# Channels on the partitions in the first product of five feed-forwards

## The chip, the cores and the metric

The kernel runs on one core of one Trainium2 chip. The metric is device time in microseconds (us), the median of several runs. Lower is better.

## The reference, cut to what matters

Two transformer blocks stand one behind the other, on 256 tokens of width 1024. They hold seven gated feed-forwards with an inner width of 2816:

```
def swiglu_ffn(h, w_in, w_out):
    a, u = jnp.split(h @ w_in, 2, axis=-1)       # 256 x 2816 each
    return (jax.nn.silu(a) * u) @ w_out          # 256 x 1024
```

The first two (first block, one for each layer) take `rmsnorm(x) @ w_ffn_in`. The other five (second block) take `swiglu_ffn(modulate(x, shift, scale), w_in, w_out)`: one on 256 context tokens, four on the latent tokens. All is float32. Beside this, the second block needs a table of modulation rows (a vector times a large matrix, here called ada), which the kernel computes piecemeal during the feed-forwards.

## The kernel before, in words

Every product is made of three TensorE passes to keep float32 precision: an operand is split into a high part in float32r and the rest, `lo = value - hi`, and the product is hi·hi + hi·lo + lo·hi. For weights, ScalarE (ACT) makes `w_hi` from the landed block `land` (L858) and GpSimd (POOL) makes `w_lo` (L766, two halves). For activations, `h_hi` and `h_lo` hold the 1024 input channels on the partitions (8 chunks `k`) and the 256 tokens on the free axis; `hid_hi` and `hid_lo` hold the inner activations in the same way (22 chunks of 128 channels).

Weights are streamed in units of 128 x 1024 float32 (512 KB), in a ring of 4 slots (`RING`). The SyncE queue (SP) issues the transfers in order and waits on `lo_ready` of the unit three before. ACT splits unit u when unit u-4 has been used (`w_used`), then POOL follows, then TensorE (PE).

The first product of a feed-forward (`ffn_in`) runs over 11 groups (`FG`) of 256 inner channels. A group takes 4 units; each unit holds two chunks k, and of each chunk 256 gate columns and 256 up columns. In `product` (L1977 to L1979) the activations are the stationary operand (128 channels x 128 tokens) and 512 weight columns are the moving one. So a group is 4 units x 2 chunks x 2 token tiles x 3 passes = 48 matmuls of 512 columns, into one PSUM bank (2 KB of each partition) per token tile; groups alternate between the bank pairs (0, 2) and (1, 3). The result has tokens on the partitions. ACT applies silu to the gate half (L993, two instructions), VectorE (DVE) multiplies with the up half into `hid` (L1556 or L1559, `gate`) and signals `taken`. Then PE turns `hid` with four 128x128 transposes (L2174, `turn_hid`), which it does one group late, after the next group's matmuls; ACT copies the turned bank to `hid_hi` (L999, `split_hid`) and DVE subtracts to make `hid_lo` (L1448, `turned_lo`).

Groups 1 to 10 run in a hardware loop, two per turn (`my.turns`). In the context feed-forward and in the first latent one, each turn also does one piece of the ada table: DVE sums eight scaled blocks (`ada_sums`, L1892, L1895), PE adds over the partitions (`ada_sum`, L2539 and L2540), DVE adds the bias (`ada_rows_out`, L1915), and SP loads the next blocks (L567), which wait on `ada_steps`, the count of DVE's steps.

The second product (`ffn_out`) has 22 units, each 12 matmuls of 512 columns over the four banks 0 to 3. It begins with three units on banks 1 and 3 alone (`HALF_FIRST`), because banks 0 and 2 are still being read for group 10; it waits on `taken`, then does the other half of the three units and turns the last `hid`.

Each engine's waits are counted by `Known`: `my.at(s, v)` is the value of semaphore `s` to wait for, and `my.up(s)` is an increment.

Of the kernel before, what the change touches and what calls it, by code (L numbers as in the profile page):

```python
# [25 lines left out]
P = 128  # L26
# [172 lines left out]
def build(nc, ins, out):  # L199
    ctx = ExitStack()  # L200
    with ctx:
# [231 lines left out]
        def forward(stages):  # L433
# [9 lines left out]
            for l in range(DEPTH):  # L443
# [29 lines left out]
                do("ffn_out", f"w_ffn_out{l}", ada=ADA_OUTS, columns=0 if last else None, then=dict(src="io", mod=(1, 0)) if last else None)  # L473
# [70 lines left out]
        def _(sp):  # L544
# [144 lines left out]
            def ffn_out(w, ada=(), columns=None, then=None):  # L689
# [150 lines left out]
        def _(act):  # L840
# [142 lines left out]
            def ffn_in(w, rms=False, ada=False, aside=False):  # L983
# [19 lines left out]
                with my.turns((FG - 1) // 2, units=8, w_used=8, taken=2, hi_ready=8, silu_ready=2, turned=2, split_hi=2,  # L1003
                              **{f"landed{s}": 32 for s in range(RING)}) as i:
# [5 lines left out]
                split_hid(FG - 1, slice(2 * (FG - 1), 2 * FG))  # L1010
# [82 lines left out]
            def ffn_out(w, ada=(), columns=None, then=None):  # L1093
# [210 lines left out]
        def _(dve):  # L1304
# [240 lines left out]
            def ffn_in(w, rms=False, ada=False, aside=False):  # L1545
# [17 lines left out]
                if aside:  # L1563
# [4 lines left out]
                            **{f"ada_in{j}": 16 for j in range(4)}) if ada else {}  # L1568
                with my.turns(times, silu_ready=2, w_used=8, taken=2, split_hi=2, split_lo=2, **sums) as i:
# [11 lines left out]
            def ffn_out(w, ada=(), columns=None, then=None):  # L1581
# [363 lines left out]
        def _(pe):  # L1945
# [222 lines left out]
            def turn_hid(g):  # L2168

                pe.wait_ge(sems["taken"], my.at("taken", n["taken"]))  # L2170
# [8 lines left out]
            def ffn_in(w, rms=False, ada=False, aside=False):  # L2179
# [5 lines left out]
                with my.turns(times, units=8, lo_ready=8, w_used=8, taken=2, split_lo=2, turned=2, **sums):  # L2185
                    for g in range(2):
                        pe.wait_ge(sems["taken"], my.at("taken", n["taken"] - 1))
                        group((1 - g, 3 - g), GW)
                        turn_hid(g)
                        n["taken"] += 1  # L2190
                    if ada:
                        ada_sum()
                        ada_at[0] += times - 1

            def ffn_out(w, ada=(), columns=None, then=None):
# [6 lines left out]
                pe.wait_ge(sems["taken"], my.at("taken", n["taken"] - 1))  # L2202
# [5 lines left out]
                pe.wait_ge(sems["taken"], my.at("taken", n["taken"]))  # L2208
                for k in range(first):
                    part(u + k, k, {0: (0,), 1: (0,)}).then_inc(*my.up("w_used"))  # L2210
                turn_hid(FG - 1)
# [417 lines left out]
```

## Time and profile before

| | |
|---|---|
| runs | 2320.15 us median of 3 (2317.98 to 2320.23) |
| the profiled execution's own time | 2314.6 us |
| its span, first to last instruction | 2312.8 us |
| mean granted TensorE clock | 0.983 of 2.4 GHz |
| PE matmul busy | 2160.7 us, 93% |
| PE weight load busy | 1747.6 us, 76% |
| POOL busy | 1700.0 us, 74% |
| ACT busy / DVE busy | 1077.4 us, 47% / 985.8 us, 43% |

The span is one execution taken by the hardware profiler. A matmul's record covers its latency: records of neighbours overlap, so the time that one costs is read from the distance between starts (its pitch) and not from its own duration. What lies outside the span is 1.8 us.

### The profile page before, as it was taken

How to read it: one execution, taken by the hardware profiler on the slowest of the kernel's cores; microseconds unless marked ns; L12 is line 12 of the kernel's file. 1: busy time of each engine (PE TensorE's matmuls, PEld its weight loads, DVE VectorE, ACT ScalarE, POOL GpSimd, SP SyncE). 2: the span in 40 equal slices, each digit the busy share in tenths (PEclk: the TensorE clock that was granted, in tenths of full speed). 3: DMA queues.
4: the chain of work that ended last, by engine and by line, in shares of the span. 5: the costliest groups of instructions: out<-in, count | busy, mean ns of one | idle time of the engine just before them, and what ended most of it. 6: DMA issues, size and time to landing. Idle time of an engine off the chain costs nothing.

```text
span 2312.8 us, 32414 instructions
## 1 busy us (share of the span) xinstructions
PE 2160.7 (93%) x10191; PEld 1747.6 (76%) x10191; DVE 985.8 (43%) x1888; ACT 1077.4 (47%) x1659; POOL 1700.0 (74%) x1367
## 2 busy tenths in 40 slices
PE   5998899999998998899999999999999999979996
PEld 4787778778877787788778777787887787766885
DVE  5555576753555454444544434454113210444112
ACT  4464344345654443444454354555444443434442
POOL 5645388777454886698888879727986988767985
PEclk9999999999999999899999999999999999999998
DMA  6434277765343778587787865524665656444663
GB/s 209 136 120 158 91 282 263 242 201 162 116 149 121 279 255 288 197 300 258 264 282 263 295 204 154 159 78 141 192 203 155 183 186 212 138 153 147 191 207 100
DMA packets 135703, 447.10 MB, mean 193 GB/s; under 512 B 22507, under 2 KB 28099, under 8 KB 135609
## 3 DMA queue, kind: packets, MB, share of 16 engines
q1 hardware_dynamic: 128920, 426.62, 56.0%
q10 hardware_dynamic: 6688, 19.23, 2.5%
q8 instruction: 58, 0.95, 0.2%
q14 instruction: 37, 0.30, 0.0%
HBM read 444.60 MB, written 3.03 MB: 194 GB/s over the span
## 4 chain that ended last, share of the span: by engine, by line
POOL 48%; issue 29%; PE 19%; DVE 1%; POOLq 1%; ACT 0%; DMA 0%; SPq 0%; ACTq 0%; DVEq 0%
POOL w_lo L766 48%; PE ps L1977 5%; PE ps L1978 5%; PE ps L1979 5%; PE ps L2438 1%; PE ps L2403 1%; PE ps L2426 1%; PE ps L2255 1%; POOLq L183 0%; PE ps L2399 0%; POOLq L764 0%; PE ps L2369 0%; PE ps L2174 0%; PE ps L2371 0%; DVE mstat L1738 0%
## 5 line engine op out<-in xcount | busy, mean ns | idle before, releaser
L766 POOL TENSOR_TENSOR w_lo<-land,w_hi 128x512 fp32r<-128x512 f32 x1308 | 1664.0, 1307 | 554.1 <-ACT w_hi L858 552.9
L858 ACT ACTIVATE w_hi<-land 128x1024 fp32r<-128x1024 f32 x654 | 691.6, 1060 | 955.7 <-PE ps L1979 706.0
L1977 PE MATMUL ps<-w_hi,h_hi 128*128 128x512 f32 (+1 forms) x1872 | 745.6, 398 | 64.9 <-DVE h_lo L1425 30.8
L1979 PE MATMUL ps<-w_hi,h_lo 128*128 128x512 f32 (+1 forms) x1872 | 732.4, 391 | 0.0
L1978 PE MATMUL ps<-w_lo,h_hi 128*128 128x512 f32 (+1 forms) x1872 | 731.8, 391 | 0.0
L1977 PEld LDWEIGHTS ps<-w_hi,h_hi 128*128 128x128 f32 x1872 | 353.7, 189 | 162.7 <-issue 45.7
L1979 PEld LDWEIGHTS ps<-w_hi,h_lo 128*128 128x128 f32 x1872 | 353.5, 189 | 75.4
L1978 PEld LDWEIGHTS ps<-w_lo,h_hi 128*128 128x128 f32 x1872 | 353.8, 189 | 68.9
L1448 DVE TENSOR_TENSOR hid_lo<-ps,hid_hi 128x512 f32 (+1 forms) x77 | 53.2, 691 | 570.3 <-ACT hid_hi L999 570.3
L1977 PE MATMUL ps<-w_hi,hid_hi 128*128 128x512 f32 x616 | 246.9, 401 | 12.9 <-POOL w_lo L766 12.9
L1978 PE MATMUL ps<-w_lo,hid_hi 128*128 128x512 f32 x616 | 244.7, 397 | 0.0
L1979 PE MATMUL ps<-w_hi,hid_lo 128*128 128x512 f32 x616 | 244.5, 397 | 0.0
L1895 DVE SCALAR_TENSOR_TENSOR ps<-ada_land,ccol,ps 128x512 f32<-128x512 f32 x322 | 230.5, 749 | 12.9 <-DMA ada_land<-ada_w_dram 4.1
L1977 PEld LDWEIGHTS ps<-w_hi,hid_hi 128*128 128x128 f32 x616 | 116.5, 189 | 45.0 <-POOL w_lo L766 16.2
L1979 PEld LDWEIGHTS ps<-w_hi,hid_lo 128*128 128x128 f32 x616 | 116.4, 189 | 28.5
L1978 PEld LDWEIGHTS ps<-w_lo,hid_hi 128*128 128x128 f32 x616 | 116.5, 189 | 27.5
L1638 DVE SCALAR_TENSOR_TENSOR ps<-ps,rows 128x512 f32<-128x512 f32 x28 | 18.6, 693 | 114.6 <-PE ps L1979 114.6
L1081 ACT ACTIVATE h_hi<-ps 128x512 fp32r<-128x512 f32 x56 | 33.1, 597 | 67.9 <-DVE ps L1416 40.2
L1977 PE MATMUL ps<-w_hi,m_hi 128*128 128x512 f32 x128 | 53.0, 414 | 4.7 <-POOL w_lo L766 3.3
L1915 DVE TENSOR_TENSOR ada_o<-ps,ada_b 2x512 f32<-2x512 f32 x36 | 24.2, 673 | 65.1 <-PE ps L2540 65.1
L1425 DVE TENSOR_TENSOR h_lo<-ps,h_hi 128x512 fp32r<-128x512 f32 x56 | 37.8, 689 | 31.6 <-ACT h_hi L1081 30.7
L1978 PE MATMUL ps<-w_lo,m_hi 128*128 128x512 f32 x128 | 50.6, 396 | 0.0
(265 smaller groups left out, 1916.7 us busy)
## 6 DMA issues: line engine op xcount, KB each, us to landing
land<-ffn_w_in_dram SPq DMA_DIRECT2D x220, 512.0 KB, 3.6
ada_land<-ada_w_dram SPq DMA_DIRECT2D x144, 512.0 KB, 5.2
land<-ffn_w_out_dram SPq DMA_DIRECT2D x110, 512.0 KB, 3.9
land<-w_ffn_in_dram SPq DMA_DIRECT2D x88, 512.0 KB, 3.9
land<-w_ffn_out_dram SPq DMA_DIRECT2D x44, 512.0 KB, 4.2
land<-na_w_qkv_dram SPq DMA_DIRECT2D x40, 512.0 KB, 4.1
land<-w_xkv_dram SPq DMA_DIRECT2D x32, 512.0 KB, 3.5
land<-w_in_dram SPq DMA_DIRECT2D x32, 488.0 KB, 3.5
```

Of the source, the lines that this page charges most:

```text
L766: done = pool.tensor_tensor(w_lo[:, slot, half], land[:, slot, half], w_hi[:, slot, half].bitcast(F32), ALU.subtract)
L858: act.activation(w_hi[:, slot, :], land[:, slot, :], ACT.Copy).then_inc(*my.up("hi_ready"))
L1081: act.activation(half_of(h_hi, i), turned_bank(i), ACT.Copy).then_inc(*my.up("split_hi"))
L1425: dve.tensor_tensor(half_of(h_lo, i), turned_bank(i), half_of(h_hi, i).bitcast(F32), ALU.subtract).then_inc(*my.up("split_lo"))
L1448: dve.tensor_tensor(lo_dst, bank(TURN + kp).rearrange("p (a b) -> p a b", a=2), hi_src.bitcast(F32), ALU.subtract).then_inc(*my.up("split_ ...
L1895: ins_ = dve.scalar_tensor_tensor(acc, w, c, acc, ALU.mult, ALU.add)
L1915: dve.tensor_tensor(ada_o[:, :], ps[0:2, ADA_OUT, :], ada_b[:, :], ALU.add).then_inc(*my.up("ada_sum"))
L1977: pe.matmul(dst, lh, wh, start=first, stop=False)
L1978: pe.matmul(dst, lh, wl, start=False, stop=False)
L1979: done = pe.matmul(dst, ll, wh, start=False, stop=last)
L2255: done = pe.transpose(ps[0:m, b, c * SEQ + t * P:c * SEQ + (t + 1) * P], tile, ident[:, :])
L2403: yield pe.matmul(s[:, t * SEQ:(t + 1) * SEQ], q[:, t * P:(t + 1) * P], k, start=(c == 0), stop=(c == len(mp["qk"]) - 1))
```

## The change

In the five feed-forwards of the second block, groups 1 to 10 exchange the operands: the weights become the stationary operand (128 input channels x 128 inner channels) and the 256 tokens of `h_hi` or `h_lo` are the moving one. The result has inner channels on the partitions, as `hid_hi` and `hid_lo` need it, so that the transposes of these groups fall away. A group is now 4 units x 2 chunks x 4 column blocks x 3 passes = 96 matmuls of 256 columns. Gate blocks (c = 0, 1) go to bank g%2, up blocks (c = 2, 3) to bank g%2 + 2. ACT's silu is one instruction of 512 elements; DVE multiplies in place in the up bank; ACT copies that bank to `hid_hi`; DVE subtracts to `hid_lo`. A bank pair is free for the next group when `split_lo` says that `hid_lo` is made, where `taken` said it before. Group 0 stays as it was, with its four transposes after group 1. The first block's two feed-forwards (`rms=True`) stay as they were. DVE's order in the ada turns moves: a turn was sums, group, group, rows out; it is now group, rows out, sums, group, with the first sums and the last rows out outside of the loop.

```diff
@@ PE, ffn_in @@
+                def group_turned(g):
+                    for j in range(4):
+                        u = n["units"]
+                        n["units"] += 1
+                        slot = u % RING
+                        pe.wait_ge(sems["lo_ready"], my.at("lo_ready", u + 1))
+                        for a in range(2):
+                            k = 2 * j + a
+                            for c in range(4):
+                                dst = ps[:, g % 2 + 2 * (c // 2), c % 2 * SEQ:(c % 2 + 1) * SEQ]
+                                at = slice(a * GW + c * P, a * GW + (c + 1) * P)
+                                pe.matmul(dst, w_lo[:, slot, at], h_hi[:, k, :], start=(k == 0 and c % 2 == 0), stop=False)
+                                pe.matmul(dst, w_hi[:, slot, at], h_hi[:, k, :], start=False, stop=False)
+                                done = pe.matmul(dst, w_hi[:, slot, at], h_lo[:, k, :], start=False, stop=(k == KC - 1 and c % 2 == 1))
+                        done.then_inc(*my.up("w_used"))
+                    n["taken"] += 1
+                pe.wait_ge(sems["taken"], my.at("taken", n["taken"] - 1))
+                group_turned(1)
+                turn_hid(0, n["taken"] - 1)
+                n["split_lo"] += 1
+                pe.wait_ge(sems["taken"], my.at("taken", n["taken"] - 1))
+                group_turned(2)
+                if ada:
+                    ada_sum()
+                with my.turns(times - 1, units=8, lo_ready=8, w_used=8, taken=2, split_lo=2, **sums):
                     for g in range(2):
-                        pe.wait_ge(sems["taken"], my.at("taken", n["taken"] - 1))
-                        group((1 - g, 3 - g), GW)
-                        turn_hid(g)
-                        n["taken"] += 1
+                        pe.wait_ge(sems["split_lo"], my.at("split_lo", n["split_lo"]))
+                        group_turned(1 - g)
+                        n["split_lo"] += 1
                     if ada:
                         ada_sum()
@@ PE, ffn_out, not rms: both waits on "taken" become waits on "split_lo", and turn_hid(FG - 1) is left out @@
@@ ACT, ffn_in @@
+                def silu_turned(g):
+                    act.wait_ge(sems["w_used"], my.next("w_used", 4))
+                    act.wait_ge(sems["taken"], my.at("taken", n["taken"]))
+                    n["taken"] += 1
+                    act.activation(flat(sg), bank(g % 2), ACT.Silu).then_inc(*my.up("silu_ready"))
+                def high(g, at):
+                    act.wait_ge(sems["taken"], my.at("taken", n["taken"]))
+                    act.activation(flat(hid_hi[:, at, :]), bank(g % 2 + 2), ACT.Copy).then_inc(*my.up("split_hi"))
...
-                    for g in (0, 1):
+                    for g in (2, 3):
                         split(4)
-                        split_hid(g, bass.ds(i * 4 + 2 * g, 2))
-                        silu(g + 1)
+                        silu_turned(g)
+                        high(g, bass.ds(i * 4 + 2 * g, 2))
@@ DVE, ffn_in @@
+                def gate_turned(g, at):
+                    dve.wait_ge(sems["silu_ready"], my.next("silu_ready"))
+                    n["w_used"] += 4
+                    up = bank(g % 2 + 2)
+                    dve.tensor_tensor(up, up, sg[:, :, :].rearrange("p t n -> p (t n)"), ALU.mult).then_inc(*my.up("taken"))
+                    dve.wait_ge(sems["split_hi"], my.next("split_hi"))
+                    dve.tensor_tensor(hid_lo[:, at, :], up.rearrange("p (a b) -> p a b", a=2), hid_hi[:, at, :].bitcast(F32),
+                                             ALU.subtract).then_inc(*my.up("split_lo"))
...
+                    with my.turns(times - 1, silu_ready=2, w_used=8, taken=2, split_hi=2, split_lo=2, **sums) as i:
+                        gate_turned(2, bass.ds(i * 4 + 4, 2))
+                        if ada:
+                            ada_rows_out()
+                            ada_sums()
+                        gate_turned(3, bass.ds(i * 4 + 6, 2))
```

## Rows read from the trace of the kernel before

**Rows 1.** The page: busy time of each engine, and the chain by engine.

```profile
PE 2160.7 (93%) x10191; PEld 1747.6 (76%) x10191; DVE 985.8 (43%) x1888; ACT 1077.4 (47%) x1659; POOL 1700.0 (74%) x1367
...
POOL 48%; issue 29%; PE 19%; DVE 1%; POOLq 1%; ACT 0%; DMA 0%; SPq 0%; ACTq 0%; DVEq 0%
```

**Rows 2.** Windows, two stages: length; PE, PEld, DVE, ACT, POOL busy; PEclk, DMA, GB/s.

```profile
986.44:1099.77 113.33, 113.33 (x520) 92.99 (x519) 45.80 (x75) 51.73 (x69) 99.26 (x80) 1.00 0.80 278
...
1807.74:1918.74 111.00, 111.00 (x509) 91.73 (x508) 13.54 (x30) 52.26 (x70) 99.22 (x80) 1.00 0.62 189
```

**Rows 3.** Timeline, PE, one group of the fourth stage: start, us, instruction.

```profile
1853.16 0.60 PE L2174 MATMUL ps<-ident,hid 128*128 128x128 f32 x4
...
1855.21 0.39 PE L1978 MATMUL ps<-w_lo,h_hi 128*128 128x512 f32 x1
...
1863.37 0.39 PE L1978 MATMUL ps<-w_lo,h_hi 128*128 128x512 f32 x1
...
1864.51 0.60 PE L2174 MATMUL ps<-ident,hid 128*128 128x128 f32 x4
```

**Rows 4.** Timeline, second product and an ada piece: PE and POOL.

```profile
1110.01 0.40 PE L1977 MATMUL ps<-w_hi,hid_hi 128*128 128x512 f32 x1
...
1110.65 12.74 POOL L766 TENSOR_TENSOR w_lo<-land,w_hi 128x512 fp32r<-128x512 f32 x10 [2.22 <-ACT w_hi L858]
...
1113.51 0.39 PE L1977 MATMUL ps<-w_hi,hid_hi 128*128 128x512 f32 x1
...
1114.21 0.40 PE L2539 MATMUL ps<-ada_hi,pick_r 128*2 128x512 f32 x1
...
1114.45 0.39 PE L2540 MATMUL ps<-ada_lo,pick_r 128*2 128x512 f32 x1
```

**Rows 5.** Timeline, PE, short plain-float32 matmuls in the attentions.

```profile
115.85 1.89 PE L2438 MATMUL ps<-zin,probT 128*128 128x64 f32 x16
...
713.27 1.89 PE L2438 MATMUL ps<-vals,probT_x 128*128 128x256 f32 x8
```

**Rows 6.** Groups by line and shape: busy us, mean ns of one.

```profile
L1979 PEld LDWEIGHTS ps<-w_hi,h_lo 128*128 128x128 f32 x1872 | 353.5, 189 | 75.4
...
L2539 PEld LDWEIGHTS ps<-ada_hi,pick_r 128*2 128x2 f32 x46 | 3.9, 84 | 9.1 <-DVE ada_lo L1904 7.0 <-issue 0.3
...
L2438 PE MATMUL ps<-zin,probT 128*128 128x64 f32 x256 | 30.5, 272 | 0.0
L2438 PE MATMUL ps<-vals,probT_x 128*128 128x256 f32 x64 | 14.8, 379 | 0.0
```

**Rows 7.** Windows and timeline, PE, 512 columns at the low clock.

```profile
925.00:929.00 4.00, 4.00 (x11) 3.12 (x10) 2.90 (x4) 1.26 (x2) 3.96 (x4) 0.50 1.02 410
...
925.28 0.63 PE L1979 MATMUL ps<-w_hi,hid_lo 128*128 128x512 f32 x1
...
929.12 0.63 PE L1979 MATMUL ps<-w_hi,hid_lo 128*128 128x512 f32 x1
```

**Rows 8.** Timeline, fourth stage, end of group 10 and behind it.

```profile
1909.92 0.60 PE L2174 MATMUL ps<-ident,hid 128*128 128x128 f32 x4
...
1911.08 0.58 ACT L999 ACTIVATE hid_hi<-ps 128x512 f32 x1
...
1911.56 0.65 ACT L993 ACTIVATE sg<-ps 128x256 f32<-128x256 f32 x2
1911.83 0.69 DVE L1448 TENSOR_TENSOR hid_lo<-ps,hid_hi 128x512 f32 x1 [10.00 <-ACT hid_hi L999]
```

**Rows 9.** Timeline, first stage, DVE and SP around an ada piece.

```profile
1020.98 0.49 PE L2174 MATMUL ps<-ident,hid 128*128 128x128 f32 x3
...
1024.76 0.73 DVE L1892 TENSOR_SCALAR ps<-ada_land,ccol 128x512 f32<-128x512 f32 x1
1025.53 5.50 DVE L1895 SCALAR_TENSOR_TENSOR ps<-ada_land,ccol,ps 128x512 f32<-128x512 f32 x7
...
1029.30 0.36 SPq L567 DMA_DIRECT2D ada_land<-ada_w_dram  x1
```

More of the change, by code:

```diff
@@ L472, in forward @@
                 last = l == DEPTH - 1
-                do("ffn_out", f"w_ffn_out{l}", ada=ADA_OUTS, columns=0 if last else None, then=dict(src="io", mod=(1, 0)) if last else None)
+                do("ffn_out", f"w_ffn_out{l}", rms=True, ada=ADA_OUTS, columns=0 if last else None, then=dict(src="io", mod=(1, 0)) if last else None)
                 do("rms", FC, gain=None if last else G_MIX + 8 * (l + 1))
@@ L687, in ffn_in, with ffn_out @@
                 stored[0] += times - 1
-            def ffn_out(w, ada=(), columns=None, then=None):
+            def ffn_out(w, ada=(), columns=None, then=None, rms=False):
                 extra = ada_extra([at - 5 for at in ada])
@@ L1091, in make_h, with ffn_out @@
                     high(i)
-            def ffn_out(w, ada=(), columns=None, then=None):
+            def ffn_out(w, ada=(), columns=None, then=None, rms=False):
                 if columns is not None:
@@ L1568, in ffn_in @@
                             **{f"ada_in{j}": 16 for j in range(4)}) if ada else {}
+                def gate_turned(g, at):
[6 more added lines that the diff above has]
+                                             ALU.subtract).then_inc(*my.up("split_lo"))
+                if not rms:
+                    if ada:
+                        ada_sums()
+                    dve.wait_ge(sems["silu_ready"], my.next("silu_ready"))
+                    n["w_used"] += 4
+                    up = bank(3)
+                    dve.tensor_tensor(up, up, sg[:, :, :].rearrange("p t n -> p (t n)"), ALU.mult).then_inc(*my.up("taken"))
+                    turned_lo(hid_lo[:, 0:2, :], hid_hi[:, 0:2, :], 0)
+                    dve.wait_ge(sems["split_hi"], my.next("split_hi"))
+                    dve.tensor_tensor(hid_lo[:, 2:4, :], up.rearrange("p (a b) -> p a b", a=2), hid_hi[:, 2:4, :].bitcast(F32),
+                                             ALU.subtract).then_inc(*my.up("split_lo"))
+                    with my.turns(times - 1, silu_ready=2, w_used=8, taken=2, split_hi=2, split_lo=2, **sums) as i:
+                        gate_turned(2, bass.ds(i * 4 + 4, 2))
+                        if ada:
+                            ada_rows_out()
+                            ada_sums()
+                        gate_turned(3, bass.ds(i * 4 + 6, 2))
+                        if ada:
+                            ada_at[0] += times - 2
+                    gate_turned(FG - 1, slice(FC - 2, FC))
+                    if ada:
+                        ada_rows_out()
+                    return
                 with my.turns(times, silu_ready=2, w_used=8, taken=2, split_hi=2, split_lo=2, **sums) as i:
@@ L1579, in ffn_in, with ffn_out @@
                 turned_lo(hid_lo[:, FC - 2:FC, :], hid_hi[:, FC - 2:FC, :], 0)
-            def ffn_out(w, ada=(), columns=None, then=None):
+            def ffn_out(w, ada=(), columns=None, then=None, rms=False):
                 for at in ada:
@@ L2184, in ffn_in @@
                 sums = dict(ada_split=1, ada_mm=1, ada_sum=1) if ada else {}
-                with my.turns(times, units=8, lo_ready=8, w_used=8, taken=2, split_lo=2, turned=2, **sums):
+                if rms:
+                    with my.turns(times, units=8, lo_ready=8, w_used=8, taken=2, split_lo=2, turned=2, **sums):
+                        for g in range(2):
+                            pe.wait_ge(sems["taken"], my.at("taken", n["taken"] - 1))
+                            group((1 - g, 3 - g), GW)
+                            turn_hid(g)
+                            n["taken"] += 1
+                        if ada:
+                            ada_sum()
+                            ada_at[0] += times - 1
+                    return
@@ L2188, in ffn_in @@
-                        group((1 - g, 3 - g), GW)
-                        turn_hid(g)
-                        n["taken"] += 1
+                        pe.wait_ge(sems["split_lo"], my.at("split_lo", n["split_lo"]))
+                        group_turned(1 - g)
+                        n["split_lo"] += 1
                     if ada:
                         ada_sum()
-                        ada_at[0] += times - 1
-            def ffn_out(w, ada=(), columns=None, then=None):
+                        ada_at[0] += times - 2
@@ L2196, in part, with ffn_out @@
+                n["split_lo"] += 1
+            def ffn_out(w, ada=(), columns=None, then=None, rms=False):
                 def part(u, k, outs):
@@ L2201, in ffn_out @@
                 first = HALF_FIRST
-                pe.wait_ge(sems["taken"], my.at("taken", n["taken"] - 1))
+                if rms:
+                    pe.wait_ge(sems["taken"], my.at("taken", n["taken"] - 1))
+                else:
+                    pe.wait_ge(sems["split_lo"], my.at("split_lo", n["split_lo"] - 1))
                 u = n["units"]
@@ L2207, in ffn_out @@
                     part(u + k, k, {0: (1,), 1: (1,)})
-                pe.wait_ge(sems["taken"], my.at("taken", n["taken"]))
+                if rms:
+                    pe.wait_ge(sems["taken"], my.at("taken", n["taken"]))
+                else:
+                    pe.wait_ge(sems["split_lo"], my.at("split_lo", n["split_lo"]))
                 for k in range(first):
                     part(u + k, k, {0: (0,), 1: (0,)}).then_inc(*my.up("w_used"))
-                turn_hid(FG - 1)
+                if rms:
+                    turn_hid(FG - 1)
                 for k in range(first, FC - 4):
```

29 lines of the change are left out of this document (25 added, 4 removed).

## The prediction

> **What bounds the kernel now.** I began with the page. PE is busy 93% of the span, POOL 74%, and yet the chain that ended last puts 48% on POOL's `w_lo` and 19% on PE [rows 1]. That chain alone would say that POOL is the limit, so the stage has to say who really waits. I laid windows over the five stages, from the first transposes to the last. In all of them PE is busy for the whole window at the full clock (113.33 of 113.33 us, 111.00 of 111.00 us); POOL is busy 99.2 us of 111.00 [rows 2]. So PE never waits, and POOL waits for a slot that PE gives back. POOL's floor is ten halves in 12.74 us, 2.55 us for a unit and 10.2 us for a group [rows 4]; PE needs 11.35 us for a group. PE's own time sets these stages, by a margin of 1.1 us a group.
>
> What is inside of those 11.35 us comes from PE's timeline. Between two transposes 11.35 us pass. Matmuls start at 1855.21 and, 36 of them later, at 1863.37: 226.7 ns each. 48 of these are 10.88 us, and so the turn of `hid` costs PE 0.47 us a group: four transposes, the refilling behind them, and a few slower matmuls [rows 3].
>
> **The change, part by part.**
>
> *The transposes go.* Ten turns in each of five feed-forwards: 50 x 0.47 = 23.5 us off PE. Nothing hides this gain, since PE is the stage's limit.
>
> *48 matmuls of 512 columns become 96 of 256.* The columns that stream are the same; what counts is the cost of one short matmul, x. There are 5 x 10 x 48 = 2,400 pairs, each costing 2x - 226.7 ns more. Break-even for the product alone is x = 113.3 ns; with the 23.5 us of the transposes it is x = 118.2. The trace has no float32r matmul of 256 columns, and this is where the prediction is decided.
>
> Lower bound: at 2.4 GHz 256 columns take 106.7 ns. In plain float32 256 columns take two clocks each: eight in 1.89 us less one duration of 0.379 make 216 ns, 213.3 and 2.5 over, with a weight load behind every one [rows 5, 6]. So a short matmul with a new stationary operand can have as little as 2.5 ns of its own. And loads limit x from below: a load of 128 columns records 189 ns, one of 2 columns 84 [rows 6], so 126 columns are 105 ns and a full load is 107 ns; 16 matmuls of only 64 columns, each with its load, come at 108 ns [rows 5, 6]. So x is at least 108 or 109.
>
> Upper bound: a float32r matmul of 512 columns takes 226.7 ns in the first product [rows 3] and 233.3 ns in the second (15 in 3.50 us, [rows 4]), 13.4 to 20 ns above the 213.3 of the bare stream. If all of this were a fixed price of an instruction, x would be 120.1 to 126.7. If it goes by columns, x is 113.3 to 116.7. What speaks for the columns: at the 1.2 GHz level (granted clock 0.50) nine matmuls take 3.84 us, 426.7 ns each, which is 512 columns and nothing over [rows 7]. The excess is only there when 4-byte columns pass at 2.4 GHz, and plain float32, which takes two clocks for a column, has 2.5 ns only. A limit on the reading of the moving operand does just that. The weight load is not its cause: the ada matmul at 1114.21 has a load of two columns behind it (84 ns) and still 0.24 us to the next [rows 4, 6]. But a fixed gap that the slower clock hides fits as well. I take x = 115.0, the middle of the column case: 2,400 x (230.0 - 226.7) = +8 us.
>
> By the Trainium skill, page "TensorE: Matmul & The Clock Gate", section "Back-to-back issue gap", a matmul costs its columns over 2.4 GHz plus 2.5 ns: 109.2 ns at 256 columns, with which the pairs would save 20 us and not cost 8. For 512 columns that rule gives 215.8 ns where this trace has 226.7 and 233.3, so it is not exact for these operands; the same section says that in a stream of loads and matmuls both set the spacing, with 81 ns at 128 columns where the bare rule has 56. That speaks against the change, since it doubles the loads; 25 ns more on x would cost 120 us.
>
> *Loads double*, from 48 to 96 a group. At 107 ns each they fit behind 113 to 117 ns of streaming, without room to spare. No pair in the trace has both near 107, so this is a risk and not a term.
>
> *ACT and DVE.* ACT: one silu of 512 in place of two of 256 (0.65 us), the same copy (0.58). DVE: two operations of 512 (0.69 each) for two of 256 and one of 512. Both lie beside PE: ACT is busy 52 us and DVE 14 to 46 us of a window [rows 2]. Their order matters where PE waits on them. Behind group 10 in the trace, ACT is free 1.16 us after PE's last matmul (1909.92 to 1911.08) [rows 8]. New: silu 0.60, multiply 0.69, copy 0.58, subtract 0.69, with 0.17 us between engines (1911.66 to 1911.83): `hid_lo` is ready 4.2 us after a group's end. Inside of the loop its bank is wanted again 11 us after, so nothing waits. At the start of the second product it is wanted after 18 matmuls, 18 x 0.233 = 4.2 us: a tie. I put 0.3 us there for wait and refilling, five times: +1.5 us. The three splits that ACT has queued behind need slots which the second product has not given back by then, so they lose nothing.
>
> *The ada pieces in two stages.* DVE's sums began 3.8 us after the group's end (1020.98 to 1024.76). Now they come behind `hid_lo` (4.2) and the rows out (some 0.7), at 4.9: 1.1 us later. SP's next ada load, and the weight transfers queued behind it, need two of the eight steps, which were done at 1026.3; SP issued it at 1029.30, 3.0 us later [rows 9]. So 1.1 us is covered; if that cover were gone the weights' transfers would be late next. Priced at nothing. POOL: at x = 115 a unit is 2.76 us of PE, and POOL's floor stays 2.55.
>
> **Sum**, against the profiled execution's own 2314.6 us: - 23.5 + 8 + 1.5 = - 14, so 2300.6 us. The runs' median is 2320.15, and the same 14 us off it make 2306.
>
> **The rivals.** Times are on the median's footing; without the pair term they start at 2320.15 - 22 = 2298.
>
> *A. The excess goes by columns (my forecast)*, x from 113.3 to 117: pair term 0 to +17.5 us, 2298 to 2316. Chance 0.45.
>
> *B. The excess is a fixed price of each float32r matmul*, x from 119 to 126.7. It speaks for it that the excess varies (13.4, 20) with unchanged columns, which a pure rate would not do. Pair term +27 to +64 us: 2325 to 2362, slower. It decides from x = 118.9 on (0.2% above). Chance 0.32.
>
> *C. Between the two*, x from 117 to 118.9: 2316 to 2325, no change. Chance 0.11.
>
> *D. The excess is a matter of long streams* and vanishes, x from 108.5 to 113, limited by the loads: pair term down to - 23 us, 2275 to 2298. The rows of the attentions speak for it (108 and 216 ns) [rows 5], those of float32r against. This is where the page's 109.2 ns would lie. Chance 0.08.
>
> *E. The loads are not hidden* when load and stream are of the same length, x from 130 to 214: pair term from +80 us, a time of 2378 and more. Against it: every load in the trace is hidden but for at most 20 ns. [...] Chance 0.04.
>
> That the change doesn't do what it says, so that PE waits for `split_lo` in every group, would take a chain of 11 us for the 4.2 us counted above; I leave it out.
>
> **How the numbers follow.** About 0.2% (4.6 us) is what a measurement of this kernel can tell from no change. Faster: A and D, 0.53. Same: C, 0.11. Slower: B and E, 0.36. Predicted 2306, from A. The range for 8 in 10 takes all of A and C, the upper half of D and of B what lies below x = 123.4 (+48 us): 2290 to 2346. A's own range is 2298 to 2316.
>
> **What would show it.** In the profile after: starts of the 128x256 matmuls in the first product, 113 to 117 ns apart (B: 120 or more; D: 112 or less; E: 130 or more); group lengths of 10.9 to 11.2 us in place of 11.35, plus the ada pieces; the transposes of `hid` (7 x 11 x 4 = 308) become 2 x 44 + 5 x 4 = 108; PE still busy for the whole window and POOL's idle time a little smaller; a wait of PE on `hid_lo` only at the head of the second product, below 0.4 us, in five places; SP's ada loads not later than before against PE. The prediction is wrong if x is 119 or more, which I can't exclude from these rows, or if DVE's chain is late in the two ada stages, which would show as PE gaps there and not in the other three.

## The result and the profile after

The changed kernel takes 2324.2 us in the median of 20 runs (2320.34 to 2333.12), the kernel before 2318.18 in 20 runs beside them. The ratio is 1.0028, 95% interval 1.0018 to 1.0038: 6 us slower, with 4.2 to 8.8 us inside of the interval. I had forecast 14 us faster. The profiled execution took 2327.98 us (span 2326.1), 13.4 more than the profiled one of before. Not all of those 13.4 us belong to the change: the first product of the first feed-forward, which the diff leaves alone, already starts 2.0 us later (at 292.2 after 290.2), the second 3.1 us later (751.4 after 748.3), and the first changed one 3.9 us later (965.1 after 961.2), before any changed group has run.

The page of the changed kernel: busy times, and the chain by engine.

```profile
PE 2173.6 (93%) x12391; PEld 1858.0 (80%) x12391; DVE 987.7 (42%) x1838; ACT 1075.7 (46%) x1609; POOL 1701.5 (73%) x1367
...
POOL 49%; issue 30%; PE 18%; DVE 1%; POOLq 1%; ACT 0%; DMA 0%; SPq 0%; ACTq 0%; DVEq 0%
```

PE does 2,200 more matmuls (10,191 before [rows 1]: 2,400 more for the pairs, 200 transposes fewer) and is busy 12.9 us longer. The chain still names POOL for nearly half; as before, that is not where the time went. Groups of the changed kernel by line and shape: busy us, mean ns of one, idle before them.

```profile
L2272 PE MATMUL ps<-h_hi,w_lo 128*128 128x256 f32 x1600 | 454.2, 284 | 6.1 <-POOL w_lo L766 6.1
L2273 PE MATMUL ps<-h_hi,w_hi 128*128 128x256 f32 x1600 | 453.1, 283 | 0.0
L2274 PE MATMUL ps<-h_lo,w_hi 128*128 128x256 f32 x1600 | 453.0, 283 | 0.0
```

1,600 of each line are 4,800 matmuls of 256 columns. Nothing makes them wait but POOL, for 6.1 us in all. Their price is read from the starts. The timeline of PE, fourth stage:

```profile
1812.12 0.28 PE L2272 MATMUL ps<-h_hi,w_lo 128*128 128x256 f32 x1
1812.24 0.28 PE L2273 MATMUL ps<-h_hi,w_hi 128*128 128x256 f32 x1
1812.36 0.28 PE L2274 MATMUL ps<-h_lo,w_hi 128*128 128x256 f32 x1
...
1813.92 0.28 PE L2272 MATMUL ps<-h_hi,w_lo 128*128 128x256 f32 x1
```

From 1812.12 to 1813.92 are 15 matmuls: 1.80 us, **x = 120.0 ns**. A pair costs 240.0 ns where one matmul of 512 columns cost 226.7 [rows 3]. The handover into the second product, where I had put 0.3 us, and the chain of ACT and DVE beside it:

```profile
1922.59 0.28 PE L2274 MATMUL ps<-h_lo,w_hi 128*128 128x256 f32 x1
1922.71 0.39 PE L2040 MATMUL ps<-w_hi,hid_hi 128*128 128x512 f32 x1
1922.94 0.40 PE L2041 MATMUL ps<-w_lo,hid_hi 128*128 128x512 f32 x1
```

```profile
1923.94 0.58 ACT L1020 ACTIVATE sg<-ps 128x512 f32<-128x512 f32 x1
...
1924.55 0.70 DVE L1604 TENSOR_TENSOR ps<-ps,sg 128x512 f32<-128x512 f32 x1 [9.29 <-ACT sg L1020]
1925.28 0.60 ACT L1025 ACTIVATE hid_hi<-ps 128x512 fp32r<-128x512 f32 x1 [0.77 <-DVE ps L1604]
1925.91 0.69 DVE L1606 TENSOR_TENSOR hid_lo<-ps,hid_hi 128x512 fp32r<-128x512 f32 x1 [0.67 <-ACT hid_hi L1025]
```

PE goes from one product into the other without a gap or a refilling, and `hid_lo` is done at 1926.60, 3.9 us after the group's end (I had counted 4.2). It is in time: no matmul behind 1922.71 waits for it. The turns are gone as counted; one tile of the changed kernel, all its matmuls:

```profile
L2237 PE MATMUL ps<-ident,hid x108: 269/272/273, 319.3 to 2141.4; 128*128 128x128 f32 x108
```

Per feed-forward, measured from the first matmul of its first product to that of the stage behind it, the two profiles give 196.7 and 198.3 us for the first of the five, 197.3 and 198.7 for the second, 200.1 and 201.6 for the fourth: +1.4 to +1.6 us each. The third has +3.3. Half of that is the clock: at 1773.87, in its second product, PE had stood 1.49 us for `w_lo`, and from 1774 to 1778 the granted clock was 0.57, where the same stretch of the kernel before has 1.00; 4 us at 0.57 cost 1.7 us. The terms with x = 120.0 say 480 pairs x 13.3 ns = 6.4, less ten turns of 0.47 = 4.7, so +1.7.

### The profile page after: what moved, and what is told of

It reads as the page before. It is cut to its first block, busy times and chain, and to the rows that moved or that the text cites. A ratio compares the mean times of both kernels' runs of the same rounds, so it can differ in the third digit from the quotient of the medians.

```text
span 2326.1 us, 36480 instructions
## 1 busy us (share of the span) xinstructions
PE 2173.6 (93%) x12391; PEld 1858.0 (80%) x12391; DVE 987.7 (42%) x1838; ACT 1075.7 (46%) x1609; POOL 1701.5 (73%) x1367
## 4 chain that ended last, share of the span: by engine, by line
POOL 49%; issue 30%; PE 18%; DVE 1%; POOLq 1%; ACT 0%; DMA 0%; SPq 0%; ACTq 0%; DVEq 0%
POOL w_lo L766 48%; PE ps L2040 3%; PE ps L2042 3%; PE ps L2041 3%; PE ps L2272 2%; PE ps L2274 2%; PE ps L2273 2%; PE ps L2546 1%; PE ps L2534 1%; PE ps L2511 1%; PE ps L2363 1%; POOLq L183 0%; PE ps L2507 0%; POOL ada_land L812 0%; POOLq L764 0%
## 5 line engine op out<-in xcount | busy, mean ns | idle before, releaser
L2040 PE MATMUL ps<-w_hi,h_hi 128*128 128x512 f32 (+1 forms) x1072 | 430.9, 402 | 58.1 <-DVE h_lo L1455 30.9
L2272 PE MATMUL ps<-h_hi,w_lo 128*128 128x256 f32 x1600 | 454.2, 284 | 6.1 <-POOL w_lo L766 6.1
L2273 PE MATMUL ps<-h_hi,w_hi 128*128 128x256 f32 x1600 | 453.1, 283 | 0.0
L2274 PE MATMUL ps<-h_lo,w_hi 128*128 128x256 f32 x1600 | 453.0, 283 | 0.0
L2042 PE MATMUL ps<-w_hi,h_lo 128*128 128x512 f32 (+1 forms) x1072 | 420.8, 393 | 0.0
L2041 PE MATMUL ps<-w_lo,h_hi 128*128 128x512 f32 (+1 forms) x1072 | 420.8, 392 | 0.0
L2272 PEld LDWEIGHTS ps<-h_hi,w_lo 128*128 128x128 f32 x1600 | 307.3, 192 | 9.6 <-issue 5.0
L2273 PEld LDWEIGHTS ps<-h_hi,w_hi 128*128 128x128 f32 x1600 | 307.3, 192 | 0.3
L2274 PEld LDWEIGHTS ps<-h_lo,w_hi 128*128 128x128 f32 x1600 | 307.3, 192 | 0.0
L2042 PEld LDWEIGHTS ps<-w_hi,h_lo 128*128 128x128 f32 x1072 | 203.6, 190 | 43.4
L2041 PEld LDWEIGHTS ps<-w_lo,hid_hi 128*128 128x128 f32 x616 | 117.1, 190 | 27.6
```

The source lines that it names most:

```text
L2040: pe.matmul(dst, lh, wh, start=first, stop=False)
L2041: pe.matmul(dst, lh, wl, start=False, stop=False)
L2042: done = pe.matmul(dst, ll, wh, start=False, stop=last)
L2272: pe.matmul(dst, w_lo[:, slot, at], h_hi[:, k, :], start=(k == 0 and c % 2 == 0), stop=False)
L2273: pe.matmul(dst, w_hi[:, slot, at], h_hi[:, k, :], start=False, stop=False)
L2274: done = pe.matmul(dst, w_hi[:, slot, at], h_lo[:, k, :], start=False, stop=(k == KC - 1 and c % 2 == 1))
```

## The experiments

Twelve kernels. Times in brackets are the kernel before, run beside them. Two theories stood at the start: the *fixed price* (every float32r matmul costs 13.3 ns over its columns, whatever their number; the prediction's B) and the *load* (now that a new stationary tile comes every 120 ns, the load sets the pace or exposes some of itself).

### The price of one matmul by itself

A kernel with TensorE alone: streams of 96 equal matmuls, one kind behind another. It leaves out the whole computation and stores its input.

```
for i in range(N): pe.matmul(ps[:, i % 4, 0:256], st[:, s(i)], xr[:, 0:256], ...)    # L57, also 128, 384, 512 (L55, L59, L61)
for i in range(N): pe.matmul(ps[:, i % 4, 0:256], st[:, 0:P], xr[:, 0:256], ...)     # L63, one stationary tile; 512: L65
for i in range(N): pe.matmul(ps[0:32, i % 4, :], st[:, 32 columns], xr[:, 0:512], ...) # L67
for i in range(N): pe.matmul(ps[:, 0, 0:256], st[:, s(i)], xr[:, 0:256], ...)        # L69, one bank
for i in range(N): pe.matmul(ps[:, i % 4, 0:256], xb[:, s(i)], xb[:, 0:256], ...)    # L73, bfloat16; 512: L75; plain float32: L71
```

> TensorE alone, nothing of the reference is computed (the output is the input x). Stretches of 96 matmuls with start distances: float32r with a new stationary operand each time at 128, 256, 384 and 512 columns; 256 and 512 columns with one stationary operand; 512 columns with a stationary operand of 32 columns; 256 columns into a single bank; plain float32 256; bfloat16 256 and 512. Theory F (the excess is a fixed price of each float32r matmul): 120 at 256, 173 at 384, 227 at 512, the same with one stationary operand and with the narrow one, and bfloat16 only 2 to 3 ns above its stream. Theory L (the price belongs to the weight load of 128 columns, which takes reading away from the stream): 227 at 512 with full loads, 215 to 217 with the narrow stationary operand. Theory C (by columns, my prediction's): 113 at 256, 170 at 384, 227 at 512; it has already lost 256 columns in the changed kernel.

Timeline of that kernel, PE, stretches of a stream: start, us from the first start to the last end, count.

```profile
29.80 1.95 PE L55 MATMUL ps<-xr,st 128*128 128x128 f32 x16
39.82 2.56 PE L57 MATMUL ps<-xr,st 128*128 128x256 f32 x20
54.70 2.59 PE L59 MATMUL ps<-xr,st 128*128 128x384 f32 x14
69.69 2.65 PE L61 MATMUL ps<-xr,st 128*128 128x512 f32 x11
89.80 1.96 PE L63 MATMUL ps<-xr,st 128*128 128x256 f32 x15
109.79 2.43 PE L65 MATMUL ps<-xr,st 128*128 128x512 f32 x10
124.67 2.71 PE L67 MATMUL ps<-xr,st 128*32 128x512 f32 x11
144.74 1.48 PE L69 MATMUL ps<-xr,st 128*128 128x256 f32 x11
169.83 1.46 PE L71 MATMUL ps<-x 128*128 128x256 f32 x6
195.76 2.46 PE L73 MATMUL ps<-xb 128*128 128x256 bf16 x21
209.66 2.54 PE L75 MATMUL ps<-xb 128*128 128x512 bf16 x11
```

The weight loads of the stream with one stationary tile:

```profile
L63 PEld LDWEIGHTS ps<-xr,st 128*128 128x128 f32 x96 | 11.7, 192 | 0.1
```

A stretch less one duration (0.283 us at 256 columns, 0.334 at 384, 0.389 at 512; bfloat16 0.273 and 0.379), over its count less one, is the price. Float32r: 256 columns (2.56 - 0.283) / 19 = 119.8 ns, 384: 173.5, 512: 226.1; over the whole streams the means are 120.5, 173.7 and 227.1. At 2.4 GHz 256, 384 and 512 columns are 106.7, 160.0 and 213.3 ns: the excess is 12.8 to 13.8 for each size, so it is a price of the instruction and not of its columns. One bank: 119.7, so the change of bank does not make it. One stationary tile all along: 119.8 and 226.8, but this says little of the load, since the tile is still loaded ahead of each of the 96 matmuls. What speaks against the load is the size: the excess is the same at 384 and 512 columns, where a load of 107 ns [rows 6] has room to spare, and a stationary tile of 32 columns, whose load is recorded with 109 ns in place of 188, gives not less but 231.6. At 128 columns it is 111.1 ns, where 53.3 + 13.3 would be 67. That fits the load of 107 ns as the limit; no stream without loads was run to show it.

13.3 ns is not the whole price everywhere. The narrow tile has 18 over its columns, and the second products have 20, before [rows 4] and after (233.3 ns at 512 columns). No run here shows what the further 5 to 7 ns are.

Bfloat16: 109.4 and 216.1 (means 109.2 and 215.8), 2.5 over. Plain float32, 256 columns: 216 ns for each of its two passes. The formula of the Trainium skill, page "TensorE: Matmul & The Clock Gate", section "Back-to-back issue gap" (columns over 2.4 GHz and 2.5 ns) agrees with the bfloat16 rows, 109.2 and 215.8; for float32r the measurement decides, and it says 13.3 in place of 2.5.

### Short matmuls with the operands of before

The kernel before, with 480 x 5 matmuls of 512 columns cut in two of 256; the activations stay stationary, and the turns stay.

```
+ for c in range(2):
+     dst = ps[:, b, c * 256:(c + 1) * 256]
+     at = slice(a * GW + c * 256, a * GW + (c + 1) * 256)
+     pe.matmul(dst, lh, w_hi[:, slot, at], ...)
+     pe.matmul(dst, lh, w_lo[:, slot, at], ...)
+     done = pe.matmul(dst, ll, w_hi[:, slot, at], ...)
```

> The kernel before with its operands as they were (activations stationary, transposes kept), but each 512-column matmul of groups 1 to 10 in the five feed-forwards split into two of 256. Theory F (fixed price for each matmul, whichever operand is stationary): 120 ns each, 2,400 x 13.3 = 32 us above before, about 2350. Theory O (the 120 ns come from the exchange of the operands: weights read by the load path, h by the stream): 113 ns each here and no more than before, 2318.

2347.79 us [2318.33], ratio 1.0133 (1.0116 to 1.0150): +29.5 us. 2,400 pairs x 13.3 ns are 31.9. PE's timeline shows the same 120 ns with the other operand stationary:

```profile
1849.82 0.28 PE L2200 MATMUL ps<-w_hi,h_lo 128*128 128x256 f32 x1
...
1850.78 0.28 PE L2199 MATMUL ps<-w_lo,h_hi 128*128 128x256 f32 x1
```

Eight in 0.96 us. Here it does not matter which operand is stationary; that there are two instructions does.

### The turns put back

The changed kernel, with the four transposes of a stale tile behind 40 of the 50 groups.

```
+ for c in range(2):
+     for t in range(T):
+         pe.transpose(ps[:, TURN, ...], hid[:, 0, t, c * P:(c + 1) * P], ident[:, :])
```

> The changed kernel with four transposes of a stale tile put back behind each of groups 3 to 10 of the five feed-forwards, 40 turns (their result is not used). If the turn's price was sized right at 0.47 us, 40 x 0.47 = 19 us above the changed kernel, about 2343. If the transposes had been cheaper than that beside the rest (the alternative for why the change lost), 40 x 0.33 = 13 us or less.

2344.41 us [2318.33], ratio 1.0114 (1.0097 to 1.0131), 20 us above the changed kernel's 2324.2: 0.5 us for a turn, where I had read 0.47 from before. The first term of my sum was right.

```profile
1865.23 0.28 PE L2274 MATMUL ps<-h_lo,w_hi 128*128 128x256 f32 x1
1865.35 0.60 PE L2292 MATMUL ps<-ident,hid 128*128 128x128 f32 x4
1865.70 0.36 PE L2272 MATMUL ps<-h_hi,w_lo 128*128 128x256 f32 x1
1865.90 0.28 PE L2273 MATMUL ps<-h_hi,w_hi 128*128 128x256 f32 x1
```

### Two passes in one instruction

`w_hi` meets `h_hi` and `h_lo` from the same stationary tile. If both lie side by side, 512 columns can pass at once. The kernel below does this in the three feed-forwards without ada pieces and sends these products to one bank; it leaves out the adding up of the two halves, and shows the price of the matmuls alone.

```
- pe.matmul(dst, w_hi[:, slot, at], h_hi[:, k, :], ...)
- done = pe.matmul(dst, w_hi[:, slot, at], h_lo[:, k, :], ...)
+ done = pe.matmul(bank(7), w_hi[:, slot, at], h_both[:, :, k, :], ...)
```

> The changed kernel, where in the three feed-forwards without ada pieces groups 1 to 10 do their two passes over w_hi as one matmul of 512 columns (h_hi beside h_lo) into a spare bank. The sum of that bank with the rest is left out, so this times the matmuls only. Same columns, 64 matmuls a group in place of 96. Theory F (13.3 ns for each float32r matmul): 3 x 10 x 32 x 13.3 = 12.8 us below the changed kernel, about 2311, and 6 to 8 below before. Theory C' (columns and loads set the time, the number of instructions nothing): as the changed kernel, 2324.

2314.5 us [2316.66], ratio 0.9986 (0.9967 to 1.0004): no change against the kernel before, where I had expected 6 to 8 us below it, and 8 to 10 us below the changed kernel (2.2 under its own kernel before, which the changed one is 6.0 above), for 960 instructions fewer (960 x 13.3 = 12.8). PE's timeline, fourth stage:

```profile
1849.76 0.28 PE L2272 MATMUL ps<-h_both,w_lo 128*128 128x256 f32 x1
...
1851.84 0.28 PE L2272 MATMUL ps<-h_both,w_lo 128*128 128x256 f32 x1
```

Six pairs of one short and one long matmul in 2.08 us are 346.7 ns each, where three short ones took 360.0: the 13.3 ns are given back with the instruction. Groups 1 to 10 took 112.8 us here in place of 117.1. In the third and the fifth stage they took 114.9: there a pair cost 353.3 ns, 6.6 more. So 8.6 of the 12.8 us came, and what the 6.6 ns are stays open.

### Cross passes in bfloat16

If a bfloat16 matmul costs 2.5 ns over its columns, two of the three passes could be made so. Both kernels, with one edit; they compute the same sums with two of three passes at bfloat16 precision. ACT makes a bfloat16 copy of `w_hi`, DVE of the activations.

```
- pe.matmul(dst, lh, wl, ...); done = pe.matmul(dst, ll, wh, ...)
+ pe.matmul(dst, lb, wl, ...); done = pe.matmul(dst, ll, wb, ...)
...
+ act.activation(w_hb[:, slot, :], w_hi[:, slot, :].bitcast(F32), ACT.Copy)
```

> The kernel before, with bfloat16 operands in the two cross passes of every weight product: w_lo and the activations' lo parts are written as bfloat16, and bfloat16 copies of the high parts are made beside (ACT one more 128x1024 copy a unit, DVE one more copy for each quarter of h, m and hid). All products are kept, two of three passes in lower precision. Theory F with the stand-alone stretches (bfloat16 costs 2.5 ns over its stream, float32r 13.3): 4,976 of 7,464 matmuls get 10.9 ns cheaper or more, 54 us or more off PE; less some 10 to 15 us for DVE's copies at the heads of the stages: about 2275. Rival: ACT, with 1.06 us more a unit, becomes late and the kernel gets slower than before.

> The changed kernel with the same bfloat16 cross passes. In the changed groups a triple of 256 columns costs 120 + 2 x 109.2 = 338.4 ns in place of 360, so a group 32 x 338.4 = 10.83 us; the unchanged order with bfloat16 has 16 x (226.7 + 2 x 215.8) + 0.47 = 11.00. So by theory F the exchange of the operands now pays: 50 x 0.17 = 8 us below bf_before, about 2267. If the price were not tied to the kind of the operand, it would lie 6 us above bf_before, as the changed kernel lies above before.

2416.84 us and 2401.16 [2316.66], ratios 1.0392 (1.0343 to 1.0440) and 1.0358 (1.0332 to 1.0383): far slower. The six times of the first lie wide apart, from 2391 to 2430 us. PE's timeline of the second, 512 columns:

```profile
1850.84 0.58 PE L2054 MATMUL ps<-w_hi,h_hi 128*128 128x512 f32 x1
1851.27 0.39 PE L2055 MATMUL ps<-w_lo,h_hb 128*128 128x512 bf16 x1
1851.49 0.38 PE L2056 MATMUL ps<-w_hb,h_lo 128*128 128x512 bf16 x1
1851.52 0.58 PE L2054 MATMUL ps<-w_hi,h_hi 128*128 128x512 f32 x1
```

A triple takes 0.68 us, as with float32r alone (3 x 226.7). 658 ns are what its three prices add up to; some 20 ns go with the change of type, which also moves the start of the float32r one forward (0.03 us behind the one ahead of it, then 0.43). That takes away what the pair of bfloat16 passes would save; most of the loss is in PE's waits: the profiled span of the first kernel is 101 us longer than that of the kernel before, and 82 of these are idle time of PE. It stood 52.6 us for the activations' copies `h_hb` (30.8 for `h_lo` before), 22.5 for `hid` in four places and 13.3 for `z` of ACT (1.5 before). Two things lie behind these, and I did not part them: ACT's added copies raise its busy time from 1077 to 1740 us, and DVE's casts of `hid_hi`, 0.42 us at the least, took over 1 us in 12 of 77 cases, up to 12.8; the next section is about such casts. My expectation had named ACT's copies as the rival, and neither the change of type nor the casts.

### One pass in bfloat16, in an order of its own

Now only the pass of `w_lo`, which needs no copy from ACT. So that the type changes once in a unit, all float32r passes come first (they wait for `hi_ready` alone) and the low pass behind them (it waits for `lo_ready`). The expectations speak of the feed-forwards; the edit covers every product with streamed weights, those of the attentions too.

```
- pe.wait_ge(sems["lo_ready"], my.at("lo_ready", u + 1))
- for a in range(2): ... w_hi by h_hi, w_lo by h_hi, w_hi by h_lo
+ for low in (False, True):
+     ready("lo_ready" if low else "hi_ready", u)
+     for a in range(2): ... (w_lo by h_hb) if low else (w_hi by h_hi, w_hi by h_lo)
...
+ dve.tensor_copy(hb_dst, hi_src.bitcast(F32)).then_inc(*my.up("split_lo"))
```

> The kernel before with all five feed-forwards' third pass alone (low part of the weights by the activations) in bfloat16, and its passes put in order: the eight float32r passes of a unit first, then its four bfloat16 passes, so one pair of type switches a unit; DVE makes the bfloat16 copies of the activations. It computes the same sums with that one pass in bfloat16. If a float32r matmul costs 13.3 ns over its columns and a bfloat16 one 2.5 (theory of the fixed price), a unit of first product goes from 12 x 226.7 = 2,720 ns to 8 x 226.7 + 4 x 215.8 + about 21 for a pair of switches = 2,698 ns, and a unit of second product saves about as much: over some 600 units about -20 us, less 10 to 15 us of copies at the heads of the stages: 2,300 to 2,312. Rival: the wait for the low part was what kept the passes apart, and copies or switches eat it: 2,318 or above.

> The kernel after with the same edit. It computes the same sums with the third pass in bfloat16. Theory of the fixed price: at 256 columns there are twice as many matmuls to save on, so a unit of 24 goes from 24 x 120.0 = 2,880 ns to 16 x 120.0 + 8 x 109.2 + about 16 = 2,810 ns; over 250 units of first product -17 us, and some -20 us in the second product, less 10 to 15 us of copies at the heads: 2,295 to 2,308, so 8 to 12 us more off than the same edit takes off the kernel before. Rival (the float32r load behind a bfloat16 matmul is exposed each time, as in the two bfloat16 kernels run before): nothing gained, 2,324 or above.

2351.12 us and 2335.9 [2319.63], ratios 1.0136 (1.0119 to 1.0154) and 1.0072 (1.0056 to 1.0088). Both slower; the expectation was wrong for both. The page says nothing of why, the waits of PE do. Of the first of them:

```profile
PE ps L2193 <- DVE hid L1566: 33.0, 5, 7.9
...
PE ps L2193 <- DVE hid L1563: 15.7, 2, 7.8
```

Seven stalls in seven feed-forwards, up to 7.9 us each, 48.7 in all. (The profiled execution was the longest of the six, 2375.73 us, so the others probably lost less.) DVE's timeline around one of them, and GpSimd's:

```profile
1649.48 14.02 DVE L1455 CAST kv<-hid_hi  x1
1663.42 0.74 DVE L1566 TENSOR_TENSOR hid<-ps,sg 128x256 f32<-128x256 f32 x2
...
1666.92 0.42 DVE L1455 CAST kv<-hid_hi  x1
```

```profile
1643.41 19.81 POOL L771 TENSOR_TENSOR w_lo<-land,w_hi 128x512 bf16<-128x512 f32 x16
```

The same cast takes 0.42 us at 1666.92 and 14.02 at 1649.48. GpSimd ran 16 subtractions without a break from 1643.41 to 1663.22; the cast ended at 1663.50, when they did. The gate that gives PE its `hid` is queued behind the cast on DVE. By the Trainium skill, page "SBUF — State Buffer", section "Who interferes with whom", a cast out of SBUF can enter a mode that needs the port pair which VectorE shares with GpSimd, and "the other **fully blocks**". That agrees with these rows, except that the page speaks of the length of one instruction, while here the cast stood through at least eleven. PE pays twice: behind the stall of 7.94 us its matmuls of 512 columns came 0.43 us apart, at the 1.2 GHz level (granted clock 0.50 from 1664 to 1668).

```profile
1664.30 1.11 PE L2193 MATMUL ps<-ident,hid 128*128 128x128 f32 x4 [7.94 <-DVE hid L1566]
...
1666.91 0.63 PE L1993 MATMUL ps<-w_hi,h_hi 128*128 128x512 f32 x1
1667.34 0.63 PE L1994 MATMUL ps<-w_hi,h_lo 128*128 128x512 f32 x1
```

### The same with another form of copy

The copy is made as a maximum of the bank in PSUM and the rounded value, with the operands of the subtraction ahead of it. It is slower when nothing disturbs it (0.68 us for 0.42).

```
- dve.tensor_copy(hb_dst, hi_src.bitcast(F32))
+ dve.tensor_tensor(hb_dst, bank(TURN + kp)..., hi_src.bitcast(F32), ALU.max)
```

> The kernel before with the low pass in bfloat16, as in the run of it before, but each bfloat16 copy of an activation is made by DVE as a two-operand maximum with the bank in PSUM and the rounded value (692 ns a half group, as the low part beside it), not as a one-operand cast out of SBUF. Theory of the port: the casts (0.42 us alone, up to 14.0 us while GpSimd's subtractions ran without a break) stand and wait on GpSimd, and with them the first gate of each feed-forward, so that TensorE stood 48.7 us in seven places; with the new form no copy lasts over 1 us, these waits vanish, and 2,351 becomes 2,305 to 2,318. Rival (DVE has simply too much to do at the heads of the stages, and a longer form makes it later still): the waits stay and the time is 2,351 or more. It computes the same sums with the third pass in bfloat16.

> The kernel after with the low pass in bfloat16 and the same new form of copy. Theory of the port: the three places in which TensorE stood 5.4 us each behind a cast go (19.0 us in the trace), and 2,336 becomes 2,310 to 2,322; the changed first products keep their 118.5 us (after: 123.9) because the bfloat16 pass costs 109.2 ns a matmul where float32r costs 120.0. Against the kernel before under the same edit it should then stand nearly even, since with a third of the passes at 2.5 ns over their columns the pair term falls from 32 us to about 24 and the turns still go. Rival (too much work on DVE): no gain, 2,336 or more. It computes the same sums with the third pass in bfloat16.

2309.49 us and 2300.32 [2319.34], ratios 0.9956 (0.9942 to 0.9970) and 0.9921 (0.9906 to 0.9935). In the first, DVE's operation of that line, count and ns min, median, max:

```profile
L1455 DVE TENSOR_TENSOR kv<-ps,hid_hi x77: 678/681/683, 327.4 to 2239.1; 128x512 f32 x70, 128x512 bf16<-128x512 f32 x7
```

For the cast it was 416/417/14023. 77 copies, none above 683 ns, and no wait of PE for `hid` is left in the list of waits. The form of the copy was the cause. That it is the port is how the Trainium skill would have it; no run here parts this from another reason. Both are now faster than the kernel before, the second by more than I had expected (2,310 to 2,322). So something else gained too.

### The order alone

The last two take bfloat16 out again: all passes in float32r, no copies, only the order of the passes and their two waits stay.

> The kernel before with only the order of the passes changed, as in the two bfloat16 kernels before it: the passes that need only the high part of the weights first, those with the low part behind them, all three passes in float32r, no copies. It computes what the kernel before computes. If the gain of 10 us came from the bfloat16 pass (216 ns instead of 227 at 512 columns), the order alone gives 2,316 to 2,322 here. Rival: it came from the order (TensorE waited 44.6 us for GpSimd's low parts before, 20.1 us with the new order), and this stands at about 2,300 to 2,312.

> The kernel after with only the order of the passes changed, all three in float32r, no copies. If the bfloat16 pass gives most (a changed first product of a unit 24 x 120.0 = 2,880 ns here, 2,790 measured with the bfloat16 pass: 5.4 us a feed-forward), the changed first products stay at 123.9 us and the whole at 2,315 to 2,322. Rival (the order gives all): 2,300 to 2,308. It computes what the kernel after computes.

**2291.82 us** and **2296.89** [2318.16], ratios 0.9886 (0.9869 to 0.9903) and 0.9907 (0.9890 to 0.9924). One of the five executions of the second took 4,327 us, the other four 2,295.65 to 2,298.66; I have no explanation for it, and the ratio leaves it out. The rival holds, and both times lie even below the ranges that I had put for it (2,300 to 2,312 and 2,300 to 2,308): the order gives all of the gain, and the bfloat16 pass with its copies had cost 16 to 18 us on top of the one and 2 to 3 on top of the other. Waits of PE in the faster of the two, and the head of one feed-forward in its timeline:

```profile
PE ps L1982 <- POOL w_lo L766: 20.3, 25, 2.8
PE ps L1984 <- DVE h_lo L1425: 16.2, 11, 7.8
PE ps L1984 <- issue: 13.7, 11, 1.8
...
PE ps L1984 <- ACT w_hi L858: 4.9, 2, 4.2
```

```profile
1768.75 0.47 PE L1984 MATMUL ps<-w_hi,h_hi 128*128 128x512 f32 x1 [0.76 <-DVE h_lo L1425]
...
1779.64 1.20 PE L1982 MATMUL ps<-w_lo,h_hi 128*128 128x512 f32 x4 [0.66 <-POOL w_lo L766]
```

The same list of the kernel before has 44.6 us for `w_lo` in 37 places and 30.8 us for `h_lo`; in the head of this feed-forward its timeline shows PE standing three times:

```profile
1788.57 0.47 PE L1977 MATMUL ps<-w_hi,h_hi 128*128 128x512 f32 x1 [0.98 <-DVE h_lo L1425]
...
1794.99 0.50 PE L1977 MATMUL ps<-w_hi,h_hi 128*128 128x512 f32 x1 [0.70 <-POOL w_lo L766]
...
1799.43 0.50 PE L1977 MATMUL ps<-w_hi,h_hi 128*128 128x512 f32 x1 [1.42 <-POOL w_lo L766]
```

POOL is the slow link while a stage fills its ring (2.55 us a unit [rows 4] against 2.72 for PE leaves it little to catch up with). In the old order PE could begin no pass of a unit before its low part was there, though two of three do not need it. With the high passes first, PE has 8 x 226.7 ns = 1.8 us of work in each unit to cover the low part. The waits named above change by - 24.3 (`w_lo`), - 14.6 (`h_lo`), + 12.1 (issue, 1.6 before) and + 4.9 (`w_hi`), - 21.9 us; others grow, so that PE's idle time falls by 18.2 us. The other 7.9 us of the 26.1 between the two profiled spans are in PE's busy time (2160.7 and 2152.8 us, the same instructions). The mean granted clock rises from 0.983 to 0.986, which would be some 7 us (0.003 x 2,313 us); whether it rises because the waits are shorter I have not tested.

Of these two kernels, too, the changed one is the slower, by 5.1 us (6.0 in this study). This is the version to take: the kernel before with the passes reordered, 1.1% below it.

## Why the prediction was wrong

**What bounds the stages** was read rightly: PE's own time set them, and a change of PE's instructions by + 8.5 us in sum showed as + 6. POOL's idle time did not set anything new (6.1 us of waits in the changed groups).

**The turns** (- 23.5 us) were right: 0.5 us each when put back, 0.47 counted.

**The pair term is the step that failed.** The mechanism and its bounds stood in the text, and the choice within them was wrong: x = 115.0, "the middle of the column case". It measured 120.0, which is the low end of rival B, and above its deciding point of 118.9. 2,400 x 13.3 ns = + 32 us in place of + 8. The row that misled me was the low clock: 426.7 ns at 512 columns and nothing over [rows 7]. I took "the excess is only there at the full clock" for "so it goes with the rate of the columns". A fixed 13.3 ns that the slower clock hides fits that row as well, as the text said itself, and the stream of 384 and 256 columns decides for it. The evidence against the column reading was there too: 226.7 and 233.3 ns for the same 512 columns [rows 3, 4] can't come from a rate alone. It was used for B and then outweighed. It speaks against one price for all as well: the 233.3 stayed after the change, and B's upper end of 126.7, worked out from them, did not come.

**The handover** (+ 1.5 us): nothing. There is no gap at the head of the second product, and the refilling that a turn had cost is gone with it.

**The loads**: hidden, as taken. At 256 columns a load of 107 ns is the closest to its stream, and the excess is no larger there than at 384 and 512.

**The ada pieces**: no gap of PE there beyond those of the other stages, as taken. The two feed-forwards with ada pieces changed by +1.6 and +1.4 us, the fourth, without, by +1.5.

**The sum** with what was measured: - 23.5 + 32 + 0 = + 8.5 us against + 6.0 (4.2 to 8.8). Of the rivals only B stands at x = 120.0.

## What to carry to other kernels

Count instructions as well as columns: in float32r each matmul cost its columns over 2.4 GHz and 13.3 ns (up to 20 in places), so cutting 512 columns into two of 256 costs 6% of the product, and what is saved by it must be more than that; where one stationary tile meets two moving operands, passing them in one instruction saves one price (what it costs to add up the two halves was not measured). Put first in each unit the passes that need only what comes first, and wait for the rest in front of the pass that needs it: this was worth 1.1% here, or 26 us, more than the 14 us that I had forecast for the change. Watch for a fast one-operand copy on VectorE beside a busy GpSimd: its median looks harmless (0.417 us), its maximum doesn't.

## What the runs showed of the hardware that I had not expected

- A float32r matmul has 13.3 ns over its columns at 256, 384 and 512 columns alike (120.0, 173.7, 227.1 ns), in one bank or four; with a stationary tile of 32 columns it was 18, and in the second products 20. Bfloat16 has 2.5 (109.2, 215.8). At 128 columns float32r takes 111.1 ns, near the 107 ns of a load.
- One change from float32r to bfloat16 and back costs some 20 ns (a triple of 512 columns took 680 ns for 658), enough to eat what a pair of bfloat16 passes saves.
- A cast from SBUF to SBUF on VectorE, 0.42 us by itself, stood up to 14.02 us while GpSimd worked without a break; the two-operand form out of PSUM never took more than 0.683 us in 77 uses.
